# The stage edges of a two-block transformer kernel: last products of tile 0 bank by bank, residual by halves, gate remainders later

## The reference, cut to what matters

```python
def swiglu(x, w_gate, w_up, w_down):
    return (jax.nn.silu(x @ w_gate) * (x @ w_up)) @ w_down

for l in range(DEPTH):                                   # first block, DEPTH = 2
    h = layer_norm(ALPHA * h + 0.5 * swiglu(h, ...ffn1), ln1_g[l], ln1_b[l])
    mix = hybrid_mixer(h, ...)                           # ends in merged @ w_out
    h = layer_norm(ALPHA * h + mix, ln2_g[l], ln2_b[l])
    h = layer_norm(ALPHA * h + 0.5 * swiglu(h, ...ffn2), ln3_g[l], ln3_b[l])

def modulated_residual(x, c, g, w_mod, b_mod, fn):       # second block, four times
    shift, scale, gate = ada_params(c, w_mod, b_mod)
    h = rms_norm_2(x, g) * (1 + scale) + shift
    return x + gate * fn(h)
```

## Time and profile before

| | us |
|---|---|
| median of 3 runs | 2815.9 (2812.65 to 2815.98) |
| the profiled execution, its own time | 2817.78 |
| its span in the trace | 2815.9 |
| TensorE busy | 2753.7 (98%) |
| VectorE busy | 2192.7 (78%) |
| ScalarE busy | 1512.1 (54%) |

### The profile page before, as it was taken

The page is one execution under the profiler, slowest core; times in us unless marked ns, Lnnn a source line. Parts: engine busy times, 40 slices in busy tenths (PEclk is TensorE's granted clock), DMA queues, the critical chain, the costliest instruction groups (busy, mean ns, idle before and its releaser), DMA issues.

```text
span 2815.9 us, 41967 instructions
## 1 busy us (share of the span) xinstructions
PE 2753.7 (98%) x15680; PEld 2361.0 (84%) x15680; DVE 2192.7 (78%) x2699; ACT 1512.1 (54%) x1690; POOL 29.7 (1%) x83
## 2 busy tenths in 40 slices
PE   8999999999999999999999999999999999999997
PEld 7889898888888999888896887858888888888886
DVE  7877886888787799788865554649889888988987
ACT  4435534454444463445432543527777776776774
POOL 2000000000000000000000000000000000000000
PEclk9999999999999999999999999999999999999999
DMA  9765422686776443268644553429999999999995
GB/s 310 246 209 175 142 102 90 233 274 231 236 256 235 165 133 121 68 223 278 227 156 154 194 193 128 142 82 355 354 347 345 348 341 350 349 337 355 336 352 200
DMA packets 407394, 659.78 MB, mean 234 GB/s; under 512 B 14410, under 2 KB 251832, under 8 KB 407288
## 3 DMA queue, kind: packets, MB, share of 16 engines
q1 hardware_dynamic: 407288, 658.32, 66.9%
HBM read 657.23 MB, written 1.05 MB: 234 GB/s over the span
## 4 chain that ended last, share of the span: by engine, by line
PE 87%; DVE 7%; DVEq 2%; ACT 2%; issue 1%; DMA 1%; SPq 0%; ACTq 0%
PE banks L810 18%; PE banks L811 18%; PE banks L812 18%; PE banks L828 12%; PE banks L829 6%; PE banks L806 2%; DVE ffn_tmp L2035 1%; PE banks L1435 1%; PE banks L912 1%; PE banks L2495 1%; PE banks L2407 1%; DVE panel_rest L1979 1%; DVE expert_rest L1317 1%; DVEq L2028 1%; PE banks L1559 1%
## 5 line engine op out<-in xcount | busy, mean ns | idle before, releaser
L810 PE MATMUL banks<-ffn_arena 128*128 128x512 f32 (+1 forms) x1988 | 747.9, 376 | 2.0 <-DVE ffn_arena L1327 1.0
L1317 DVE TENSOR_TENSOR expert_rest<-expert_raw,ffn_arena 128x2048 fp32r<-128x2048 f32 (+1 forms) x306 | 647.0, 2161 | 81.1 <-ACT ffn_arena L1142 76.6
L812 PE MATMUL banks<-ffn_arena 128*128 128x512 f32 (+1 forms) x1924 | 709.8, 369 | 0.0
L1142 ACT ACTIVATE ffn_arena<-expert_raw 128x2048 fp32r<-128x2048 f32 (+1 forms) x306 | 539.3, 1815 | 64.0 <-PE banks L812 53.6
L828 PE MATMUL banks<-ffn_arena 128*128 128x512 f32 x1440 | 510.5, 398 | 0.5 <-DVE ffn_arena L1223 0.5
L811 PE MATMUL banks<-expert_rest,ffn_arena 128*128 128x512 f32 (+1 forms) x1216 | 461.6, 380 | 0.0
L810 PEld LDWEIGHTS banks<-ffn_arena 128*128 128x128 f32 x1988 | 374.4, 188 | 70.3 <-issue 2.7
L812 PEld LDWEIGHTS banks<-ffn_arena 128*128 128x128 f32 x1924 | 362.6, 188 | 69.8
L829 PE MATMUL banks<-ffn_arena 128*128 128x256 f32 x1440 | 404.3, 281 | 0.0
L828 PEld LDWEIGHTS banks<-ffn_arena 128*128 128x128 f32 x1440 | 270.6, 188 | 67.6 <-issue 1.1
L810 PE MATMUL banks<-ffn_arena,mix_high 128*128 128x256 f32 x984 | 280.8, 285 | 1.7 <-DVE panel_rest L1979 1.7
(11 more groups left out here) (461 smaller groups left out, 3938.9 us busy)
## 6 DMA issues: line engine op xcount, KB each, us to landing
expert_raw<-in_moe_w_gate_dram SPq DMA_DIRECT2D x90, 1024.0 KB, 5.1
expert_raw<-in_moe_w_up_dram SPq DMA_DIRECT2D x90, 1024.0 KB, 5.3
expert_raw<-in_moe_w_down_dram SPq DMA_DIRECT2D x90, 1024.0 KB, 5.1
gate_w<-in_ffn_w_gate_dram SPq DMA_DIRECT2D x55, 1024.0 KB, 5.2
up_w<-in_ffn_w_up_dram SPq DMA_DIRECT2D x55, 1024.0 KB, 5.2
down_w<-in_ffn_w_down_dram SPq DMA_DIRECT2D x55, 1024.0 KB, 5.1
mod_unit<-in_mod_w_dram SPq DMA_DIRECT2D x48, 1024.0 KB, 5.2
panel<-in_w_in_dram SPq DMA_DIRECT2D x48, 1024.0 KB, 5.3
```

Source lines behind the costliest of these rows:

```text
L810: mm(out, w[0], x[0], start=start, stop=False)
L812: return mm(out, w[1], x[0], start=False, stop=stop)
L1142: act_fn(high[:, half, :], tile[:, half, :], ACT.Copy).then_inc(expert_hi, 1 if h else 1 + skipped)
L1317: tt(rest[:, half, :], tile[:, half, :], high[:, half, :].bitcast(F32), ALU.subtract).then_inc(expert_lo, 1 if h else 1 + skipped)
```

## The change

It touches the places where one stage ends and the next begins.

- The last down products of an FFN, of tile 0 only, run bank by bank: all products of bank 0 (columns 0 to 511), then all of bank 1. Each bank ends with an increment of `tile_done`, which now counts two for each edge. The output products of the mixer, of the convolution and of the attention are treated in the same way.
- VectorE's residual of tile 0, with its layer norm statistics, runs in two halves, each behind its bank. The second block's residual does so too (`residual_halves`).
- The first gate panel of an FFN: its products run in three rounds over both output blocks, high by high, then high weights by the rows' remainders, then the gate's remainders by high rows. The last 16 matmuls are the only ones to need `gate_low`. The two output blocks are in two banks (1 and 2, in the second block's FFN 0 and 1), and silu reads both with one instruction.
- VectorE makes the first gate panel's remainders behind those of the rows, before the up panel's, and no longer before the layer norm. At the kernel's start they are moved the same way.

```diff
@@ -799,7 +799,9 @@
 
 
         mm = nc.tensor.matmul
-        FIRST_BANK = 1
+        def first_bank(n):
+            return 0 if n == 2 * DEPTH * NS else 1
+
 
         def turn(out, tile):
             k = tile.shape[0]
@@ -845,23 +847,27 @@
         def down_block(units, weights, f, t, start, stop):
 
             for c in range(2):
-                last = split_mm(banks[:, 2 * t + c, :], [u[:, f, t * P:(t + 1) * P] for u in units],
-                                [w[:, f, c * 512:(c + 1) * 512] for w in weights], start, stop)
+                last = down_half(units, weights, f, t, c, start, stop)
             return last
 
+        def down_half(units, weights, f, t, c, start, stop):
+            return split_mm(banks[:, 2 * t + c, :], [u[:, f, t * P:(t + 1) * P] for u in units],
+                            [w[:, f, c * 512:(c + 1) * 512] for w in weights], start, stop)
+
         def ffn_down_last(pe, n, last_down):
 
-            for t in range(TT):
+            for c in range(2):
                 for s, units, weights in ((NS - 2, unit_parts, down_parts), (NS - 1, last_unit_parts, last_down)):
-                    if t == 0:
-                        pe.wait_ge(down_low, n + s + 2)
-                        pe.wait_ge(act_ready, n + s + 1)
+                    pe.wait_ge(down_low, n + s + 2)
+                    pe.wait_ge(act_ready, n + s + 1)
+                    for f in range(FB):
+                        last = down_half(units, weights, f, 0, c, False, s == NS - 1 and f == FB - 1)
+                last.then_inc(tile_done, 1)
+            for t in range(1, TT):
+                for s, units, weights in ((NS - 2, unit_parts, down_parts), (NS - 1, last_unit_parts, last_down)):
                     for f in range(FB):
                         last = down_block(units, weights, f, t, False, s == NS - 1 and f == FB - 1)
-                    if t == TT - 1:
-                        last.then_inc(down_done, 1)
-                    elif s == NS - 1:
-                        last.then_inc(tile_done, 1)
+                    last.then_inc(down_done, 1)
 
         def ffn_down(pe, n, s, first=False, final=False, units=unit_parts, weights=down_parts, width=SEQ):
             pe.wait_ge(down_low, n + s + 2)
@@ -874,19 +880,19 @@
 
         def ffn_gate_first(pe, n, x_done):
 
-            pe.wait_ge(gate_low, n + 2)
+            pe.wait_ge(gate_high, (n + 1) * 2)
             pe.wait_ge(silu_done, n + 1)
             pe.wait_ge(x_high, x_done)
             high, low = gate_parts
-            for f in range(FB):
-                out_, cols = banks[:, FIRST_BANK, f * SEQ:(f + 1) * SEQ], slice(f * P, (f + 1) * P)
-                for k in range(KD):
-                    mm(out_, high[:, k, cols], x_parts[0][:, k, :], start=k == 0, stop=False)
-                    mm(out_, low[:, k, cols], x_parts[0][:, k, :], start=False, stop=False)
-                if f == 0:
+            for i, (w, x) in enumerate(((high, x_parts[0]), (high, x_parts[1]), (low, x_parts[0]))):
+                if i == 1:
                     pe.wait_ge(x_low, x_done)
-                for k in range(KD):
-                    last = mm(out_, high[:, k, cols], x_parts[1][:, k, :], start=False, stop=k == KD - 1)
+                elif i == 2:
+                    pe.wait_ge(gate_low, n + 2)
+                for f in range(FB):
+                    for k in range(KD):
+                        last = mm(banks[:, first_bank(n) + f, 0:SEQ], w[:, k, f * P:(f + 1) * P], x[:, k, :],
+                                  start=i == 0 and k == 0, stop=i == 2 and k == KD - 1)
             last.then_inc(gate_done, 1)
 
         def ffn_pe(pe, n, f, last_down=last_down_parts):
@@ -1093,7 +1099,10 @@
         def silu_act(act, n, s, width, bank=4):
             act.wait_ge(gate_done, n + s + 2)
             act.wait_ge(unit_ready, n + s + 1)
-            act_fn(ffn_tmp[:, 0:width], banks[:, bank, 0:width], ACT.Silu).then_inc(silu_done, 1)
+            if bank < 4:
+                act_fn(v3(ffn_tmp, 0, FB, SEQ), banks[:, bank:bank + FB, 0:SEQ], ACT.Silu).then_inc(silu_done, 1)
+            else:
+                act_fn(ffn_tmp[:, 0:width], banks[:, bank, 0:width], ACT.Silu).then_inc(silu_done, 1)
 
         def rest_act(act, dst, bank):
             act_fn(v3(ffn_tmp, dst, FB, SEQ), banks[:, bank:bank + FB, SEQ:], ACT.Copy).then_inc(rest_copied, 1)
...
@@ -1369,13 +1378,18 @@
 
             for t in range(TT):
                 if t == 0:
-                    dve.wait_ge(tile_done, m)
+                    for half in range(2):
+                        cols = slice(half * 512, (half + 1) * 512)
+                        dve.wait_ge(tile_done, 2 * m - 1 + half)
+                        stt(H[:, t, cols], H[:, t, cols], scale, acc[:, t, cols], ALU.mult, ALU.add)
+                        dve.drain()
+                        nc.vector.bn_stats(stats[:, t, half, :], H[:, t, cols])
                 else:
                     dve.wait_ge(*whole)
-                stt(H[:, t, :], H[:, t, :], scale, acc[:, t, :], ALU.mult, ALU.add)
-                dve.drain()
-                for half in range(2):
-                    nc.vector.bn_stats(stats[:, t, half, :], H[:, t, half * 512:(half + 1) * 512])
+                    stt(H[:, t, :], H[:, t, :], scale, acc[:, t, :], ALU.mult, ALU.add)
+                    dve.drain()
+                    for half in range(2):
+                        nc.vector.bn_stats(stats[:, t, half, :], H[:, t, half * 512:(half + 1) * 512])
                 dve.drain()
                 nc.vector.bn_aggr(moments[:, t, :], stats[:, t, :, :])
                 dve.drain().then_inc(var_ready, 1)
@@ -1729,17 +1743,33 @@
                 out_pair(4, 17, moT_parts, j)
...
+                                    [w[:, k % 2, c * 512:(c + 1) * 512] for w in weights], i == 0 and k == 0, i == 1 and k == 3)
+
+                def out_ready_pe(k):
+                    half_ready(2 * SPLIT_USES.index(18 + i) + k // 2)
+                    pe.wait_ge(out_low, l * OUT_PARTS + 6 + (4 * i + k) // 2 + 1)
+
+                if i == 0:
                     for k in range(4):
-                        if t == 0 and k % 2 == 0:
-                            half_ready(2 * SPLIT_USES.index(18 + i) + k // 2)
-                            pe.wait_ge(out_low, l * OUT_PARTS + 6 + (4 * i + k) // 2 + 1)
-                        weights = mix_half(2 * SPLIT_USES.index(18 + i) + k // 2)[:0:-1]
+                        if k % 2 == 0:
+                            out_ready_pe(k)
                         for c in range(2):
-                            last = split_mm(banks[:, 2 * t + c, :], [m[:, 4 * i + k, t * P:(t + 1) * P] for m in merged_parts],
-                                            [w[:, k % 2, c * 512:(c + 1) * 512] for w in weights], i == 0 and k == 0, i == 1 and k == 3)
-                    if i == 1:
-                        last.then_inc((tile_done, mix_done)[t], 1)
+                            project_out(0, k, c)
+                else:
+                    for c in range(2):
+                        for k in range(4):
+                            if c == 0 and k % 2 == 0:
+                                out_ready_pe(k)
+                            last = project_out(0, k, c)
+                        last.then_inc(tile_done, 1)
+                for k in range(4):
+                    for c in range(2):
+                        last = project_out(1, k, c)
+                if i == 1:
+                    last.then_inc(mix_done, 1)
...
@@ -2742,20 +2777,17 @@
 
             for l in range(DEPTH):
                 n = l * FFN_LAYER
-                if l == 0:
-                    gate_vec(dve, n, 0)
                 turned_vec(dve, l * 2)
+                gate_vec(dve, n, 0)
                 if l:
                     dve.wait_ge(mod_col_done, l * 2)
                 ffn_vec(dve, n, l * 2)
                 layer_norm(dve, l * LN_LAYER + 1, 2 * ALPHA, (down_done, n + NS + 1))
                 mixer_vec(dve, l)
-                gate_vec(dve, n + NS, 0)
                 layer_norm(dve, l * LN_LAYER + 2, ALPHA, (mix_done, l + 1))
                 turned_vec(dve, l * 2 + 1)
+                gate_vec(dve, n + NS, 0)
                 ffn_vec(dve, n + NS, l * 2 + 1, LAST_DOWN[l])
-                if l + 1 < DEPTH:
-                    gate_vec(dve, n + FFN_LAYER, 0)
                 if l == DEPTH - 1:
                     norm_start(0)
                 layer_norm(dve, l * LN_LAYER + 3, 2 * ALPHA, (down_done, n + 2 * NS + 1))
@@ -2779,6 +2811,15 @@
                 dve.wait_ge(grow_ready, j + 1)
                 if j + 1 < 4:
                     norm_start(j + 1)
+
+            def residual_halves(j):
+                for half in range(2):
+                    cols = slice(half * 512, (half + 1) * 512)
+                    dve.wait_ge(tile_done, 2 * (NORMS + j) + half + 1)
+                    tt(ffn_tmp[:, cols], acc[:, 0, cols], gate_row[:, cols], ALU.mult)
+                    dve.drain()
```

(36 more changed lines are left out.)

4 lines of the change are left out of this document (3 added, 1 removed).

## The result

The changed kernel takes 2826.12 us (median of 7 runs, 2823.95 to 2828.46), the kernel before 2815.98 in the 7 runs beside it (2812.65 to 2820.43): ratio 1.0034, 95% interval 1.0023 to 1.0046, about 10 us slower. The forecast was 2817.7 within 2811.5 to 2823.5, with 0.84 on no measurable change. The time lies outside the range, and the kernel is measurably slower. The profiled execution of the changed kernel took 2823.95 us, with a span of 2822.2.

A forecast was written before the change was run, and what follows sets the result against it. TensorE, busy 98% of the span, was taken as the bound. 4.0 us lost less 2.2 gained gave +1.8: profiled 2817.78 became 2819.6, less 1.9 for the median, 2817.7 us; range 2811.5 to 2823.5.

The forecast's parts named there:

- the order by bank I cost at nothing: Tile 0's last down products: reordering by bank costs nothing, since 15680 products already have 15680 weight loads.
- The bound of 0.3 us at each of five FFNs: Upper bound for order by bank and silu over two banks, from cutting a VectorE pass: 1.5 us in all.
- The gains: At the stage edges, tile 0's earlier residual and statistics shorten TensorE's waits, 2.2 us in sum.
- The mechanisms named: At the edges: no wait before the transposes at 203; tile 1's residual 0.42 us behind its last product.
- The losses of the late remainders: Gate remainders made later delay TensorE at two mixer edges, the start and the second block's FFN: 4.0 us.
- The mixer edges: Mixer to second FFN, layers 0 and 1: second gate panel's remainders end later, 0.5 us lost each.
- The start: Start of the kernel: third gate load and third up remainders move later with nil slack, 1.6 us lost.
- The second block's FFN: There the second gate panel is issued later, so its first product starts at 1559.3 instead of 1557.93: 1.4 us lost.
- The prediction's own signs of being wrong: No TensorE waits on L1223 near 51, 541, 1251 and 1559, or other clock stretches at half.
- The loads come late: Rival: late-issued gate panels land in 8.5 instead of 5.2 us at three places, 9.3 more, 2827.0; chance 0.04.
- The rival: Clock rival: new waits let the clock fall in one more stretch of 10.2 us, losing 5.1, 2822.8; chance 0.05.
- The prediction's remark that the trace disagrees at the convolution's edge: At the conv output's edge TensorE is busy 2.84 of 6.60 us, yet the granted clock stays 1.00.

The follow-up runs named there:

- the edges alone: Kernel with both edits (twelve products ahead, early remainders), but gate remainders late at the two mixer to second FFN edges: 2818.14 us, ratio 1.0003.
- the order alone: Kernel before with only tile 0's products of the last two down steps run bank by bank; no halves, no late remainders: 2827.2 us, ratio 1.0027.
- remainders put back: Changed kernel with the first gate panel's remainders made where the kernel before makes them, three rounds kept: 2821.45 us, ratio 1.0013.

## Why the prediction was wrong

**The step that failed** is "the order by bank I cost at nothing, since each product already loads its own weights". It asked what a product costs and not what stands between a product and the thing it waits for. The reordered loop holds two waits for act_ready; moving the second from behind twelve products to behind six shortens the cover from 2.7 to 1.4 us. The kernel before already waited 0.6 us in the first FFN with all twelve, a row that its list of waits shows. In the four others that list shows no such wait, yet with six ahead the waits are 1.16 to 1.35 us of the 1.4 taken away, so there too the cover had hardly any slack. The chain it had to cover lasts 2.2 us, from the multiplication's start to the dependent product's (192.68 to 194.90). The bound of 0.3 us at each of five FFNs was drawn from the cut of a VectorE pass, the wrong resource: measured are 7.1 us of waits and 7.6 us of time for this edit alone, slow products included, and 5.8 beside the other edits. Added to the forecast that is 2823.5 to 2825.3, against 2826.1.

**The gains**, 2.2 us. Six kernels with the halves, full cover and early remainders at the mixer edges have ratios of 0.9992 to 0.9997, 0.8 to 2.3 us below the kernel before; each interval reaches 1. The term agrees with these times, which are too close to the kernel before to show it. The mechanisms named are in the trace: no wait before the transposes at 203, tile 1's residual right behind its products.

**The losses of the late remainders**, 4.0 us. Measured are 3.6 between two medians of one chip (0.0012 by the ratios), but nothing in sum when they are tried place by place, so the size stays open. The waits are spread differently than said. The mixer edges, 0.5 each: waits of 0.69 in layer 0, in layer 1 0.34 in the first profile, 1.41 when the changed kernel ran again and 1.37 with the edges alone, so up to three times the term. The start, 1.6: the third up remainders start at 49.45 instead of 48.62, 0.8 us later, since the third gate panel's slipped by 0.9 only; in the runs this time does not show. The second block's FFN, 1.4: no wait appeared. That panel's remainders ended at 1555.99 in the kernel with only this place late, 13.0 us after the FFN's first product at 1543.00; in the kernel before the second panel's first product came 11.84 us after the first (1546.09 to 1557.93), which would have left the wait of 1.2 that was forecast. But in that profile, as in all with early remainders but two, it came 13.0 to 13.1 us after, because the first panel ran partly at a lower clock (its 48 products took 7.48 us, against 6.24 in the kernel with only the mixer edges late, where the second panel came 11.84 us after). The wait was hidden by slower products, which the prediction did not have; that the 1.4 us did not come says nothing against its sum. The prediction's own signs of being wrong were met in part: no wait near 1559, and this stretch at half clock, which the kernel before does not have.

**The rivals.** "The loads come late" gave 2827.0, nearly the right time for a wrong reason: the second gate panel was issued at 530.46 and ScalarE took it up at 535.66, 5.2 us later, as the sum had it. The clock did not fall at any of the changed kernel's five new waits (granted clock 1.00 in the 10 us around each), but it did behind the first of them in the kernel with the order alone. The rival has something in it: 1.2 us in the second block's FFN and 3.2 in the kernel with the order alone, and not 5.1. None of the rivals had the mechanism that decided. The second error is that the chances followed the sum: 0.84 on no change while three reordered loops and their waits had been looked at for VectorE's sake only.

## What to carry to other kernels

When a loop over banks or tiles is turned outside in, write down for each wait in it how many instructions stand ahead of it before and after, and how long the chain it waits for is; where a short wait is in the profile already, there is no slack, and each product taken from in front costs up to its full duration (0.23 us here), in every stage that runs the loop. Where no wait shows, compare the products ahead with the chain: there can be as little slack. Put only the work whose inputs are long ready in the coarse order first, and the fine order behind the wait: that kept the halves and lost nothing. An early finish is worth only what the next load or the other tile's chain lets through; here nine edges gave some 1 to 2 us of 2816 at most, and no version tried is faster than the kernel before by more than the runs can tell.

## What was not expected of the hardware

Where a stretch at 1.2 GHz stands depends on more than the code around it. In the FFN of the second block the kernel before has none, and neither has the kernel with late remainders at the mixer edges alone; the profiles of the twelve others (the changed kernel's two among them) have a short one, kernels with the same code there included. The kernel before, behind its wait of 2.17 us, and the one with the order alone, behind the same wait of 2.17 us:

```profile
1546.00:1550.00 4.00, 3.91 (x30) 3.74 (x31) 4.00 (x4) 3.98 (x5) 0.00 (x0) 1.00 0.00 0
```

```profile
1550.00:1554.00 4.00, 2.44 (x11) 2.47 (x12) 3.91 (x6) 4.00 (x8) 0.00 (x0) 0.68 0.00 0
```

From the FFN's first product to the second panel's first it is 13.02 us against 11.84: 1.2 us more, where the nearest edit upstream is at the wait that ended at 1421.68, 130 us earlier. And behind the new wait in the first FFN, 2.44 us, the clock fell in the kernel with the order alone. Behind those of 2.47 us (remainders put back), 2.51 and 2.58 (the changed kernel twice) it did not; the last of them:

```profile
193.70:203.90 10.20, 7.63 (x34) 6.36 (x35) 6.07 (x10) 2.12 (x3) 0.00 (x0) 1.00 0.68 219
```

The Trainium skill, "TensorE: Matmul & The Clock Gate", section "HAM oscillation — how this bites in real kernels", says that idle gaps between bursts of matmuls throttle the clock again. The gaps that this section speaks of are longer than these waits. So the waits without a fall agree with it, and the fall behind 2.44 us does not. The prediction's remark that the trace disagrees at the convolution's edge does not hold against it either, since the longest gap there is 2.17 us. A difference of 1 to 2 us at one place between single profiles of this kernel can therefore not be read as the effect of an edit, unless a wait with its releaser stands beside it.
